# Prompt attention in another block order, and cached rope columns turned by VectorE instead of TensorE

## The chip, the cores and the metric

The kernel is one launch on one core of a Trainium2 chip, in 32-bit floating point. The metric is device time in microseconds (us), the median of three runs. Five engines work side by side and wait for each other through semaphores only: TensorE (PE in the profile; PEld are its weight loads), VectorE (DVE), ScalarE (ACT), GpSimd (POOL) and SyncE (SP), which issues most of the transfers.

## The reference, cut to what matters

One layer of a decoder: a prompt of 512 tokens and, beside it, 8 sequences with 4 new tokens each over 4096 cached ones. The change touches two parts of it.

```python
# prompt: causal attention, 8 heads, 128 queries at a time; 64 latent-derived + 32 rope dimensions
s = (einsum('bqhd,bkhd->bhqk', qn_b, k_nope) + einsum('bqhr,bkr->bhqk', qr_b, kr)) * MLA_SCALE
s = where(kpos <= qpos, s, -inf)
o = einsum('bhqk,bkhd->bqhd', softmax(s), v)
# new tokens: attention over the paged cache, rows of 256 latent + 32 rope numbers
past = cache_l[page_table].reshape(Bd, -1, 288)
s_past = einsum('bthc,bkc->bhtk', q_lat, past[..., :256]) + einsum('bthr,bkr->bhtk', q_rope, past[..., 256:])
p = softmax(concat([s_past, s_new]) * MLA_SCALE)
ctx = einsum('bhtk,bkc->bthc', p[..., :n_past], past[..., :256]) + (the new rows' part)
```

## The kernel before

Every engine runs one written-out program in order. After the input projection, the recurrent branch and the memory's keys and values, the program comes to the two stages of this change; behind them follow the output projection, the memory attention and the MLP. All weight products go through one helper (line 544), which splits each 32-bit operand in two parts and makes three products.

**Prompt attention.** The 8 heads are taken in four pairs, and each pair has 8 steps: for block i = 0, 1, 2, 3 of 128 queries first the even, then the odd head, so 32 steps n in all. Block i sees i + 1 key tiles of 128 keys, which sets the width of everything in its step (128 to 512 columns). TensorE's program for step n is: the scores of block n (line 816) into one of three PSUM banks, the transposes of the probabilities of block n-3 (line 824), into the banks `T_BANK` in turn, and, on every second step, the values of block n-5 for both heads (line 838, 64 columns for each head) into `O_BANK`. VectorE adds the causal mask on the diagonal tile (1827), takes the negated maximum (1828), and for the block before it the reciprocal of the sum (1833) and the scaling (1834). ScalarE makes the exponentials (1397) and copies the transposed probabilities of block n-3 to SBUF (1405). Three blocks of scores can be open at once, since the scores of n wait for the exponentials of n-3.

Between these lies other work, tied to the step number. `k_pair(j)` on TensorE makes the keys of the next pair of heads and `k_copy(j)` on ScalarE takes them to SBUF, both at the first step of a pair. At the end of a pair ScalarE casts the output (`act_hi`, line 1412) and VectorE makes the remainder (`act_lo`, line 1842), both in their step n = m + 6 for the pair's last block m. From step 18 on the work for the new tokens is mixed in: `absorb_turn` (TensorE, line 770, steps 18 to 24) turns the weights w_uk through one bank, which ScalarE empties into `wukT` (1416) before the next of four goes in; `absorb` (line 778, step 27) makes the latent queries; `new_rows` (lines 789 to 794, step 30) scores the new rows. VectorE clears `qropez` (line 1799) and fills it with the rope queries: 128 rows, 8 sequences x 128 columns, where rows 32j to 32j+31 hold a sequence's queries in columns 32j to 32j+31 and zeros elsewhere.

**The page loop.** The cache is gathered in 16 halves of a sequence (n = 0 to 15): an indirect transfer from GpSimd (line 479) brings 2048 rows of 288 numbers into one of four buffers `pg`, 16 rows to a partition. For each, TensorE runs `turn(n+1)`, `turn_p(n)`, `score(n+1)`, `values(n)`:

- `turn` transposes the page (line 865), nine tiles of four 128x128 transposes each, into the four banks of `gps` in turn; ScalarE (1430) copies the even tiles to SBUF and VectorE (1851) the odd ones. The first tile holds the rope columns, which GpSimd has packed into `ropc` (line 489) so that four groups of 32 numbers fill 128 rows; the other eight are the latent columns, for `cT`.
- `turn_p` transposes the probabilities (line 891), VectorE copies them (1868).
- `score` makes one product of `ropT` with the zero-padded `qropez` over 512 columns (line 876), which writes all 128 output rows, and adds eight products with 32 weight columns each (line 881), in four column tiles of the array, for the latent part.
- `values` makes 16 products of 256 columns in the same four tiles (line 901).

VectorE takes the maximum of the scores (1860, 1861), then copies its tiles of the next page. ScalarE makes the exponentials (1443). Each 32-bit product stands in the trace as two records (passes), each with its own weight load; a transpose stands as one.

The first page's tiles follow straight on the prompt attention; four of the banks come free from it one by one, each with a wait of its own:

```python
                    if k >= 4:
                        pe.wait_ge((g_ta, g_td)[k % 2], (k - 2) // 2 if k % 2 == 0 else (k - 3) // 2)
                    elif k != 2:
                        pe.wait_ge((at_pT, new_act, None, at_lo)[k], (4 * H, 2, None, 4)[k])
```

Of the kernel before, what the change touches and what calls it, by code (L numbers as in the profile page):

```python
# [14 lines left out]
F32 = mybir.dt.float32  # L15
# [53 lines left out]
MLP_AT = {m: i for i, m in enumerate(MLP)}  # L69

# [15 lines left out]
def build(nc, x_prompt, x_sample, cache_mla, cache_mem_k, cache_mem_v, state_lru_h, state_conv, page_table,  # L86
# [7 lines left out]
    with ctx:  # L94
# [103 lines left out]
        ropT = at("ropT", [128, 512], F32, M0 + 34816)  # L198
# [7 lines left out]
        ropc = at("ropc", [128, 4, 128], F32, M0 + 39488)  # L206
# [75 lines left out]
        ropc_ok = sem("ropc_ok")  # L282
# [168 lines left out]
        def _(pool):  # L451
# [31 lines left out]
            def rope_part(n):  # L483
                pool.wait_ge(page_in[n % 4], 16 * (n // 4) + 16)
                if n == 0:
                    pool.wait_ge(new_pe, 1)
                else:
                    pool.wait_ge(g_T, 9 * n - 8)
                nc.gpsimd.tensor_scalar(ropc[:, :, :].rearrange("p i (j r) -> p j i r", j=4),
                                        pg[n % 4][:, :, CR:ROW].rearrange("p (j i) r -> p j i r", j=4), 1.0, 1.0,  # L490
                                        ALU.mult, ALU.mult).then_inc(ropc_ok, 1)
            for u in range(U_MLP + len(MLP)):
                n = 384 if U_QU <= u < U_UV else 1024
                if u == U_OUT:
# [6 lines left out]
                    pool.wait_ge(tile_done, T_OUT)  # L501
                    pool.wait_ge(wk_T, 4)
# [28 lines left out]
        def _(pe):  # L531
# [275 lines left out]
            for n in range(4 * H + 5):  # L807
                if n < 4 * H:
                    h, i = 2 * (n // 8) + n % 2, n % 8 // 2
                    if n % 8 == 0 and n // 8 + 1 < 4:  # L810
                        k_pair(n // 8 + 1)
# [7 lines left out]
                if 0 <= m < 4 * H:  # L819
# [3 lines left out]
                    for kt in range(m % 8 // 2 + 1):  # L823
                        mm = nc.tensor.transpose(T_BANK[m % 2][:, 128 * kt:128 * kt + 128],
                                                 pb[m % 4][:, 128 * kt:128 * kt + 128], ident[:, :])
                    mm.then_inc(at_T, 1)
                m = n - 5
                if m >= 0 and m % 2:
                    j, i = m // 8, m % 8 // 2
# [19 lines left out]
            def turn(n):  # L849

                pe.wait_ge(page_in[n % 4], 16 * (n // 4) + 16)
                pe.wait_ge(ropc_ok, n + 1)
                for i in range(9):
                    k = 9 * n + i
                    if k >= 4:
                        pe.wait_ge((g_ta, g_td)[k % 2], (k - 2) // 2 if k % 2 == 0 else (k - 3) // 2)
                    elif k != 2:
                        pe.wait_ge((at_pT, new_act, None, at_lo)[k], (4 * H, 2, None, 4)[k])
                    for z in range(4):
                        if i == 0:  # L860
                            src = ropc[:, z, :]
                        else:
                            c, j = divmod(i - 1, 4)
                            src = pg[n % 4][:, 4 * j + z, 128 * c:128 * c + 128]
                        mm = nc.tensor.transpose(gps[:, (k + 1) % 4, 128 * z:128 * z + 128], src, ident[:, :])  # L865
                    mm.then_inc(g_T, 1)

            def score(n):
# [5 lines left out]
                k = 9 * n  # L874
                pe.wait_ge((g_ta, g_td)[k % 2], k // 2 + 1)
                nc.tensor.matmul(out, qropez[:, b, :], ropT[:, :], start=True, stop=False, skip_group_check=True)  # L876
                for c in range(2):
                    for j in range(4):
                        k = 9 * n + 1 + 4 * c + j
                        pe.wait_ge((g_ta, g_td)[k % 2], k // 2 + 1)  # L880
                        mm = nc.tensor.matmul(out[32 * j:32 * j + 32, :], qlat[:, c, b, :],  # L881
                                              cT[:, c, 512 * j:512 * j + 512], start=False, stop=(c == 1),
# [1174 lines left out]
```

## Time and profile before

| what | value |
|---|---|
| median of 3 runs | 1060.57 us (1059.52 to 1063.98) |
| the profiled execution | 1060.25 us, span of its trace 1058.1 us |
| PE busy | 1003.6 us, 95% of the span |
| DVE, ACT, POOL busy | 515.5, 303.5, 453.7 us |
| prompt attention | 218.8 to 284.0 us of the trace |
| page loop | 284.0 to 431 us |

A matmul's duration in the trace holds its way through the array, so that records overlap: the time of a row of matmuls is read from start to start. Idle time of an engine is given with what ended it.

### The profile page before, as it was taken

Reading aid. Unit: us, or ns where it says so; the run is one execution under the profiler, and the core shown is the slowest. Engines: PE = TensorE matmul, PEld = TensorE weight load, DVE = VectorE, ACT = ScalarE, POOL = GpSimd, SP = SyncE. Lnnn points to the kernel's source line nnn. Section 1 sums busy time; section 2 is a strip of 40 time slices with the busy share of each in tenths; the row PEclk is TensorE's granted clock in tenths of the full one; section 3 lists DMA queues with packets and bytes.
Section 4 is the critical chain, followed back from the end, with each engine's and each line's share of the span. In section 5 each row is a group of like instructions: output and inputs, shape, how many; then the busy total and the mean of one; then the engine's idle time right before and its main releaser. Section 6 shows DMA issues by size and latency. Waiting matters only on the chain.

```text
span 1058.1 us, 19047 instructions
## 1 busy us (share of the span) xinstructions
PE 1003.6 (95%) x8116; PEld 897.0 (85%) x8116; DVE 515.5 (49%) x723; ACT 303.5 (29%) x619; POOL 453.7 (43%) x297
## 2 busy tenths in 40 slices
PE   4999989888999999899999899999999999999997
PEld 4989888755666666699985599999999999999996
DVE  3889887567455555366135346441243134214413
ACT  5333256366334444112025312210020011001212
POOL 3545567600111111365510045565565565555651
PEclk9999999999899999999999999999999999999999
DMA  6423344520556664542267022332322323323222
GB/s 177 129 60 81 99 137 133 144 90 31 213 199 265 258 266 172 203 140 80 61 251 267 2 60 81 88 92 81 97 84 84 97 80 90 91 80 97 84 80 85
DMA packets 144009, 129.78 MB, mean 123 GB/s; under 512 B 13093, under 2 KB 136882, under 8 KB 140086
## 3 DMA queue, kind: packets, MB, share of 16 engines
q1 hardware_dynamic: 138344, 87.99, 27.8%
q0 software_dynamic: 2304, 37.75, 9.2%
q10 hardware_dynamic: 3278, 2.83, 0.8%
q8 instruction: 64, 1.05, 0.4%
q14 instruction: 19, 0.16, 0.0%
HBM read 123.53 MB, written 5.03 MB: 122 GB/s over the span
## 4 chain that ended last, share of the span: by engine, by line
PE 80%; DVE 11%; ACT 3%; issue 2%; DMA 1%; POOL 1%; ACTq 1%; DVEq 0%; POOLq 0%
PE gps L544 55%; PE gps L865 6%; PE aux L881 3%; PE aux L901 2%; PE gps L992 1%; PE gps L1067 1%; PE aux L876 1%; POOL wlo L474 1%; PE aux L816 1%; DVE q L1788 1%; PE aux L1005 1%; PE gps L668 1%; PE gps L838 1%; DMA wraw<-in_w_mem_v_dram 1%; PE aux L1026 1%
## 5 line engine op out<-in xcount | busy, mean ns | idle before, releaser
L544 PE MATMUL gps<-act_hi,whi 128*128 128x272 f32 x944 | 274.6, 291 | 6.4 <-DVE act_lo L1564 4.1
L544 PE MATMUL gps<-act_lo,whi 128*128 128x272 f32 x944 | 273.8, 290 | 0.0
L544 PE MATMUL gps<-act_hi,wlo 128*128 128x272 f32 x944 | 273.2, 289 | 0.0
L461 POOL TENSOR_SCALAR whi<-wraw 128x1024 fp32r<-128x1024 f32 (+1 forms) x110 | 114.7, 1043 | 368.8 <-PE gps L544 316.0
L464 POOL TENSOR_TENSOR wlo<-wraw,whi 128x1024 fp32r<-128x1024 f32 (+1 forms) x110 | 260.6, 2369 | 9.2
L544 PE MATMUL gps<-h_hi,whi 128*128 128x272 f32 x640 | 185.8, 290 | 0.0
L544 PE MATMUL gps<-h_lo,whi 128*128 128x272 f32 x640 | 185.2, 289 | 0.0
L544 PE MATMUL gps<-h_hi,wlo 128*128 128x272 f32 x640 | 184.7, 289 | 0.0
L544 PEld LDWEIGHTS gps<-act_hi,whi 128*128 128x128 f32 x944 | 178.7, 189 | 6.9 <-issue 5.1
L544 PEld LDWEIGHTS gps<-act_hi,wlo 128*128 128x128 f32 x944 | 178.7, 189 | 0.0
L544 PEld LDWEIGHTS gps<-act_lo,whi 128*128 128x128 f32 x944 | 178.5, 189 | 0.0
L1902 DVE TENSOR_TENSOR XT<-gps,XT 128x544 f32<-128x544 f32 x48 | 34.8, 725 | 181.5 <-PE gps L544 181.5
L544 PEld LDWEIGHTS gps<-h_hi,whi 128*128 128x128 f32 x640 | 120.7, 189 | 0.4
L544 PEld LDWEIGHTS gps<-h_hi,wlo 128*128 128x128 f32 x640 | 120.7, 189 | 0.1
L544 PEld LDWEIGHTS gps<-h_lo,whi 128*128 128x128 f32 x640 | 120.6, 188 | 0.0
L1510 ACT ACTIVATE ms<-mr 128x544 f32<-128x544 f32 x32 | 21.1, 660 | 287.2 <-DVE mr L1982 287.2
L479 POOL DMA_INDIRECT pg<-in_cache_mla_dram,idx x16 | 16.5, 1031 | 149.4 <-PE aux L901 88.0
L1988 DVE TENSOR_TENSOR act_lo<-ms,act_hi 128x544 fp32r<-128x544 f32 x29 | 58.7, 2024 | 40.8 <-ACT act_hi L1514 40.8
L865 PE MATMUL gps<-ident,pg 128*128 128x128 f32 x512 | 58.7, 273 | 0.0
L474 POOL TENSOR_TENSOR wlo<-wraw,whi 128x512 fp32r<-128x512 f32 x32 | 46.9, 1490 | 23.0 <-ACT whi L1220 23.0
L865 PEld LDWEIGHTS gps<-ident,pg 128*128 128x128 f32 x512 | 56.4, 142 | 0.2 <-DVE act_lo L1842 0.2
L1851 DVE COPY cT<-gps 128x512 f32<-128x512 f32 x64 | 44.2, 691 | 23.0 <-PE gps L865 23.0
(356 smaller groups left out, 1479.2 us busy)
## 6 DMA issues: line engine op xcount, KB each, us to landing
wraw<-in_w_up_dram SPq DMA_DIRECT2D x32, 512.0 KB, 4.1
wraw<-in_w_down_dram SPq DMA_DIRECT2D x32, 512.0 KB, 3.9
wraw<-in_w_in_dram SPq DMA_DIRECT2D x14, 512.0 KB, 3.9
kv<-in_cache_mem_k_dram SPq DMA_DIRECT2D x7, 1024.0 KB, 7.0
kv<-in_cache_mem_v_dram SPq DMA_DIRECT2D x7, 1024.0 KB, 12.6
wraw<-in_w_mem_k_dram SPq DMA_DIRECT2D x8, 512.0 KB, 4.0
wraw<-in_w_mem_v_dram SPq DMA_DIRECT2D x8, 512.0 KB, 3.8
wraw<-in_w_out_dram SPq DMA_DIRECT2D x8, 512.0 KB, 4.8
```

The lines of the kernel that those rows point to most:

```text
L461: nc.gpsimd.tensor_scalar(whi[:, slot, 0:n], wraw[:, slot, 0:n], 1.0, 1.0, ALU.mult, ALU.mult).then_inc(pool_step, 1)
L464: nc.gpsimd.tensor_tensor(wlo[:, slot, 0:n], wraw[:, slot, 0:n], whi[:, slot, 0:n].bitcast(F32), ALU.subtract).then_inc(w_ready, 1)
L474: ins = nc.gpsimd.tensor_tensor(wlo[:, slot, part], wraw[:, slot, part], whi[:, slot, part].bitcast(F32), ALU.subtract)
L479: nc.gpsimd.indirect_dma_start(pg[n % 4][:, :, :].rearrange("p k d -> p (k d)"), None, rows_of_pages, bass.IndirectOffsetOnAxis(ap=idx[:, ...
L544: mm = nc.tensor.matmul(out_of(a), w_of(w, k), x_of(x, k, part), start=(k == 0 and s == 0), stop=(k == k_tiles - 1 and s == 2))
L865: mm = nc.tensor.transpose(gps[:, (k + 1) % 4, 128 * z:128 * z + 128], src, ident[:, :])
L881: mm = nc.tensor.matmul(out[32 * j:32 * j + 32, :], qlat[:, c, b, :], cT[:, c, 512 * j:512 * j + 512], start=False, stop=(c == 1), skip_gr ...
L901: mm = nc.tensor.matmul(aux[32 * j:32 * j + 32, 3, 0:256], pTs[:, 128 * i + 32 * j:128 * i + 32 * j + 32], pg[n % 4][:, 4 * j + i, 0:CR], ...
L1510: nc.scalar.activation(ms[:, n % 2, :], mr[:, n % 2, :], ACT.Square).then_inc(mlp_sq, 1)
L1851: V.tensor_copy(dst, gps[:, (k + 1) % 4, :]).then_inc(g_td, 1)
L1902: step(V.tensor_tensor(x, gps[:, 2 * (t % 2):2 * (t % 2) + 2, 0:HALF], x, ALU.add))
L1988: V.tensor_tensor(hidden(n)[1], ms[:, n % 2, :], hidden(n)[0].bitcast(F32), ALU.subtract).then_inc(mlp_lo, 1)
```

## The change

The order of the query blocks in a pair of heads becomes 2, 3, 1, 0. The keys of the next pair are made at steps 3, 11 and 17 instead of 0, 8 and 16. ScalarE's cast of a pair's output comes one step later, VectorE's remainder two. The clearing of `qropez` goes from VectorE to GpSimd.

The rope columns no longer pass through TensorE: VectorE transposes them in 32x32 blocks from the page buffer to `ropT` (`rope_turned`), and GpSimd's packing falls away. A page has eight tiles left to turn. The rope score becomes 16 products of 128 columns with 32 weight columns, behind the latent ones, with an output pattern in four pieces of 32. The first page's tiles wait accordingly.

```diff
+ORDER = (2, 3, 1, 0)
-        ropT = at("ropT", [128, 512], F32, M0 + 34816)
+        ropT = at("ropT", [128, 16, 32], F32, M0 + 34816)
-        ropc = at("ropc", [128, 4, 128], F32, M0 + 39488)
@@ GpSimd
-            def rope_part(n):
-                pool.wait_ge(page_in[n % 4], 16 * (n // 4) + 16)
-                if n == 0:
-                    pool.wait_ge(new_pe, 1)
-                else:
-                    pool.wait_ge(g_T, 9 * n - 8)
-                nc.gpsimd.tensor_scalar(ropc[:, :, :].rearrange("p i (j r) -> p j i r", j=4),
-                                        pg[n % 4][:, :, CR:ROW].rearrange("p (j i) r -> p j i r", j=4), 1.0, 1.0,
-                                        ALU.mult, ALU.mult).then_inc(ropc_ok, 1)
                     pool.wait_ge(tile_done, T_OUT)
+                    nc.gpsimd.memset(qropez[:, :, :], 0.0).then_inc(pool_set, 1)
                     pool.wait_ge(wk_T, 4)
                     gather(1)
                     pool.wait_ge(ql_ps, 1)
                     gather(2)
-                    rope_part(0)
                     pool.wait_ge(at_lo, 4)
                     gather(3)
-                    for i in range(NH):
-                        if i + 1 < NH:
-                            rope_part(i + 1)
-                        if i >= 1 and i + 3 < NH:
-                            pool.wait_ge(g_V, i)
-                            gather(i + 3)
+                    for i in range(NH - 4):
+                        pool.wait_ge(g_V, i + 1)
+                        gather(i + 4)
@@ TensorE, prompt attention
-                    h, i = 2 * (n // 8) + n % 2, n % 8 // 2
-                    if n % 8 == 0 and n // 8 + 1 < 4:
+                    h, i = 2 * (n // 8) + n % 2, ORDER[n % 8 // 2]
+                    if n in (3, 11, 17):
                         k_pair(n // 8 + 1)
@@ TensorE, turn(n)
-                pe.wait_ge(ropc_ok, n + 1)
-                for i in range(9):
-                    k = 9 * n + i
+                for i in range(8):
+                    k = 8 * n + i
                     if k >= 4:
-                        pe.wait_ge((g_ta, g_td)[k % 2], (k - 2) // 2 if k % 2 == 0 else (k - 3) // 2)
-                    elif k != 2:
-                        pe.wait_ge((at_pT, new_act, None, at_lo)[k], (4 * H, 2, None, 4)[k])
+                        pe.wait_ge((g_ta, g_td)[k % 2], (k - 4) // 2 + 1)
+                    else:
+                        pe.wait_ge((at_pT, new_act, at_lo, at_lo)[k], (4 * H, 2, 3, 4)[k])
@@ TensorE, score(n)
-                nc.tensor.matmul(out, qropez[:, b, :], ropT[:, :], start=True, stop=False, skip_group_check=True)
                 for c in range(2):
                     for j in range(4):
-                        k = 9 * n + 1 + 4 * c + j
+                        k = 8 * n + 4 * c + j
                         pe.wait_ge((g_ta, g_td)[k % 2], k // 2 + 1)
...
+                pe.wait_ge(g_rope, n + 1)
+                for g in range(4):
+                    for j in range(4):
+                        mm = nc.tensor.matmul(
+                            out[32 * j:32 * j + 32, :].rearrange("p (i g k) -> p g i k", i=4, g=4)[:, g, :, :],
+                            qropez[:, b, 32 * g:32 * g + 32], ropT[:, 4 * j:4 * j + 4, :], start=False, stop=(g == 3),
+                            skip_group_check=True)
                 mm.then_inc(g_S, 1)
@@ ScalarE, prompt attention
-                    if n % 8 == 0 and n // 8 + 1 < 4:
+                    if n in (3, 11, 17):
                         k_copy(n // 8 + 1)
-                m = n - 6
+                m = n - 7
                 if m >= 0 and m % 8 == 7:
@@ VectorE, prompt attention
                 if n == 18:
                     dve.wait_ge(tile_done, T_UK + 4)
-                    step(V.memset(qropez[:, :, :], 0.0))
+                    dve.wait_ge(pool_set, 9)
-                m = n - 6
+                m = n - 8
                 if m >= 0 and m % 8 == 7:
@@ VectorE, page loop
+            def rope_turned(n):
+
+                dve.wait_ge(page_in[n % 4], 16 * (n // 4) + 16)
+                V.transpose(ropT[:, :, :], pg[n % 4][:, :, CR:ROW]).then_inc(g_rope, 1)
+
+            dve.wait_ge(at_pv, 2 * H)
+            rope_turned(0)
             turned(0)
...
                 if n < NH - 1:
+                    rope_turned(n + 1)
                     turned(n + 1)
```

## Rows read from the trace of the kernel before

**Rows 1.** The page: busy time of PE, and the chain that ended last.

```profile
PE 1003.6 (95%) x8116; PEld 897.0 (85%) x8116; DVE 515.5 (49%) x723; ACT 303.5 (29%) x619; POOL 453.7 (43%) x297
...
PE 80%; DVE 11%; ACT 3%; issue 2%; DMA 1%; POOL 1%; ACTq 1%; DVEq 0%; POOLq 0%
PE gps L544 55%; PE gps L865 6%; PE aux L881 3%; PE aux L901 2%; PE gps L992 1%; PE gps L1067 1%; PE aux L876 1%; POOL wlo L474 1%; PE aux L816 1%; DVE q L1788 1%; PE aux L1005 1%; PE gps L668 1%; PE gps L838 1%; DMA wraw<-in_w_mem_v_dram 1
```

**Rows 2.** Windows: stretch, length, busy PE, PEld, DVE, ACT, POOL, granted clock, DMA.

```profile
218.80:284.00 65.20, 56.46 (x381) 38.55 (x381) 44.46 (x142) 36.66 (x113) 2.49 (x3) 0.95 0.21 79
...
263.00:274.00 11.00, 11.00 (x61) 8.14 (x63) 4.38 (x14) 2.20 (x8) 0.94 (x1) 0.69 0.90 354
302.00:428.00 126.00, 125.91 (x1268) 85.53 (x1264) 64.42 (x105) 53.48 (x108) 25.44 (x29) 1.00 0.62 234
```

**Rows 3.** Timeline of one page in the loop: start us, duration us, instruction.

```profile
319.93 0.66 PE L865 MATMUL gps<-ident,ropc 128*128 128x128 f32 x4
...
321.06 0.69 DVE L1851 COPY cT<-gps 128x512 f32<-128x512 f32 x1 [1.84 <-PE gps L865]
...
323.68 0.69 DVE L1851 COPY cT<-gps 128x512 f32<-128x512 f32 x1 [0.18 <-PE gps L865]
...
323.92 0.60 PE L891 MATMUL aux<-ident,ps 128*128 128x128 f32 x4
...
324.36 1.02 PE L876 MATMUL aux<-ropT,qropez 128*128 128x512 f32 x2
...
325.31 1.93 PE L881 MATMUL aux<-cT,qlat 128*32 128x512 f32 x16
...
327.05 1.91 PE L901 MATMUL aux<-pg,pTs 128*32 128x256 f32 x32
...
328.03 0.15 DVE L1861 TENSOR_SCALAR nm<-sl 128x1 f32<-128x1 f32 x1
...
328.89 0.66 PE L865 MATMUL gps<-ident,ropc 128*128 128x128 f32 x4
```

**Rows 4.** Timeline: runs of short passes elsewhere, with few weight columns.

```profile
234.70 1.09 PE L838 MATMUL gps<-pT,vn 128*64 128x128 f32 x16
...
237.87 0.44 PE L838 MATMUL gps<-pT,vn 128*64 128x128 f32 x4
...
428.17 0.33 PEld L925 LDWEIGHTS aux<-sl,ident 128*32 128x32 f32 x8 [0.17 <-issue]
...
431.63 0.21 PE L938 MATMUL aux<-wt,ident 32*32 32x2 f32 x7
...
436.78 1.13 PE L962 MATMUL aux<-ctxa,wuv 128*64 128x32 f32 x32 [0.88 <-DVE ctxa L1893]
```

**Rows 5.** Line 1922: durations in ns (min, median, max) and form.

```profile
L1922 DVE RECIPROCAL rsn<-rsn x2: 3553/3553/3553, 495.2 to 664.1; 128x544 f32<-128x544 f32 x2
```

**Rows 6.** Timeline of the attention stage and the first page.

```profile
246.84 0.91 DVE L1799 MEMSET qropez<- 128x1024 f32 x1 [0.16 <-issue]
...
277.10 1.13 PE L816 MATMUL aux<-Kb,q 96*128 96x512 f32 x2
...
282.94 1.09 PE L838 MATMUL gps<-pT,vn 128*64 128x128 f32 x16 [0.46 <-ACT pT L1405]
...
284.70 0.69 DVE L1842 TENSOR_TENSOR act_lo<-gps,act_hi 128x512 fp32r<-128x512 f32 x1 [3.54 <-ACT act_hi L1412]
285.31 0.68 DVE L1851 COPY cT<-gps 128x512 f32<-128x512 f32 x1
```

**Rows 7.** Waits in the attention stage: total us, times, longest.

```profile
PEld gps L770 <- ACT wukT L1416: 3.6, 3, 1.5
...
DVE act_lo L1842 <- ACT act_hi L1412: 2.6, 3, 1.0
```

More of the change, by code:

```diff
@@ L822, in _ @@
                         pe.wait_ge(at_pT, m - 1)
-                    for kt in range(m % 8 // 2 + 1):
+                    for kt in range(ORDER[m % 8 // 2] + 1):
                         mm = nc.tensor.transpose(T_BANK[m % 2][:, 128 * kt:128 * kt + 128],
@@ L873, in score @@
                     pe.wait_ge(g_exp, n - 1)
-                k = 9 * n
-                pe.wait_ge((g_ta, g_td)[k % 2], k // 2 + 1)
-                nc.tensor.matmul(out, qropez[:, b, :], ropT[:, :], start=True, stop=False, skip_group_check=True)
                 for c in range(2):
                     for j in range(4):
-                        k = 9 * n + 1 + 4 * c + j
+                        k = 8 * n + 4 * c + j
                         pe.wait_ge((g_ta, g_td)[k % 2], k // 2 + 1)
-                        mm = nc.tensor.matmul(out[32 * j:32 * j + 32, :], qlat[:, c, b, :],
-                                              cT[:, c, 512 * j:512 * j + 512], start=False, stop=(c == 1),
-                                              skip_group_check=True)
+                        nc.tensor.matmul(out[32 * j:32 * j + 32, :], qlat[:, c, b, :],
+                                         cT[:, c, 512 * j:512 * j + 512], start=(c == 0), stop=False,
+                                         skip_group_check=True)
[5 more added lines that the diff above has]
+                            qropez[:, b, 32 * g:32 * g + 32], ropT[:, 4 * j:4 * j + 4, :], start=False, stop=(g == 3),
+                            skip_group_check=True)
                 mm.then_inc(g_S, 1)
@@ L1388, in _ @@
             k_copy(0)
-            for n in range(4 * H + 6):
+            for n in range(4 * H + 7):
                 if n < 4 * H:
-                    if n % 8 == 0 and n // 8 + 1 < 4:
+                    if n in (3, 11, 17):
                         k_copy(n // 8 + 1)
-                    w = 128 * (n % 8 // 2 + 1)
+                    w = 128 * (ORDER[n % 8 // 2] + 1)
                     act.wait_ge(at_nm, n + 1)
@@ L1424, in turned @@
             def turned(n):
-                for i in range(9):
-                    k = 9 * n + i
-                    if k % 2 == 0:
-                        act.wait_ge(g_T, k + 1)
-                        dst = ropT[:, :] if i == 0 else cT[:, (i - 1) // 4, 512 * ((i - 1) % 4):512 * ((i - 1) % 4) + 512]
-                        nc.scalar.copy(dst, gps[:, (k + 1) % 4, :]).then_inc(g_ta, 1)
+                for k in range(8 * n, 8 * n + 8, 2):
+                    act.wait_ge(g_T, k + 1)
+                    i = k % 8
+                    nc.scalar.copy(cT[:, i // 4, 512 * (i % 4):512 * (i % 4) + 512], gps[:, (k + 1) % 4, :]).then_inc(g_ta, 1)
             def keep_ctx(n):
@@ L1820, in absorbed @@
                     V.tensor_scalar(nmn[:, :], sn[:, 0, :], -1.0, None, ALU.mult).then_inc(new_dve, 1)
-            for n in range(4 * H + 6):
+            for n in range(4 * H + 8):
                 if n < 4 * H:
-                    w = 128 * (n % 8 // 2 + 1)
+                    w = 128 * (ORDER[n % 8 // 2] + 1)
                     dve.wait_ge(at_s, n + 1)
@@ L1845, in turned @@
             def turned(n):
-                for i in range(9):
-                    k = 9 * n + i
-                    if k % 2:
-                        dve.wait_ge(g_T, k + 1)
-                        dst = ropT[:, :] if i == 0 else cT[:, (i - 1) // 4, 512 * ((i - 1) % 4):512 * ((i - 1) % 4) + 512]
-                        V.tensor_copy(dst, gps[:, (k + 1) % 4, :]).then_inc(g_td, 1)
+                for k in range(8 * n + 1, 8 * n + 8, 2):
+                    dve.wait_ge(g_T, k + 1)
+                    i = k % 8
+                    V.tensor_copy(cT[:, i // 4, 512 * (i % 4):512 * (i % 4) + 512], gps[:, (k + 1) % 4, :]).then_inc(g_td, 1)
+            def rope_turned(n):
[3 more added lines that the diff above has]
+            rope_turned(0)
             turned(0)
```

23 lines of the change are left out of this document (10 added, 13 removed).

## The prediction

> **What bounds the kernel now.** I read the page first [rows 1]: TensorE (PE) is busy 95% of the span and carries 80% of the chain that ended last. A shorter VectorE (DVE) or GpSimd (POOL) instruction is therefore worth nothing unless PE waits for it. Over half of the chain is line 544, the weight products, which the change leaves alone. It touches two stages: the prompt attention (218.8 to 284 us) and the loop over 16 half-sequences of cached pages (284 to 431 us).
>
> The table by windows [rows 2] tells them apart. In the page loop PE is busy 125.91 of 126 us and DVE 64.42: PE is the bound, at the full clock. In the attention stage PE is busy 56.46 of 65.2 us and DVE 44.46: neither is full, so waits matter. In the 11 us from 263 to 274 the granted clock averages 0.69, so part of that stretch runs at 1.2 instead of 2.4 GHz.
>
> The timeline of one page [rows 3] is the page loop's price list, read from start to start on PE: turning nine tiles 3.99 us (319.93 to 323.92, 0.44 a tile), turning the probabilities 0.44, the rope score 0.95, the latent scores 1.74, the values 1.84. That makes 8.96 us a page.
>
> **Change 1, the rope columns leave TensorE's turning.** Each page loses one of nine tiles: -0.44 us. The POOL instruction that packed the rope columns goes too; POOL was behind nobody's wait here, so that is worth nothing, and its gathers still wait for the same values. In return DVE gets one 128x512 transpose a page, and the rope score, which was two PE passes over 512 columns with 128 weight columns, becomes 16 matmuls of 128 columns with 32 weight columns, so 32 passes, in four 32-column tiles of the array.
>
> *What 32 short passes cost.* The latent scores have the same four tiles with 512 columns: four rounds of four side by side in 1.74 us, 0.435 a round [rows 3]. The values have 256 columns: eight rounds in 1.84 us, 0.230 a round, where half of 0.435 would be 0.218. So a change of weights adds 0.012 us a round. For 128 columns the nearest row is line 838, with two tiles of 64 weight columns: 16 passes take 1.09 us and 4 take 0.44, so six rounds cost 0.65, 0.108 a round [rows 4]. A round of 128 columns with four tiles is then 0.108 to 0.121 us, and eight rounds 0.87 to 0.97. The old score's two passes were two rounds of 512, 0.87. (The rest of its 0.95, about 0.08, is the step from the whole array to tiles; it moves to the border between the probabilities' turn and the latent scores.) I take 0.12 us more. Can PE start passes that fast? 32 of them in 0.97 us are 30 ns each. Line 962 runs 32 passes in 1.13 us, of which the last is about 0.22: 29 ns each, with 64 weight columns. Line 938 runs 7 passes in 0.21 us, of which the last is 0.17 [rows 4]. So issue is not the limit. What no row shows is four tiles of 128 rows of the array with loads only 128 columns apart. The least it can cost is 0 over the old score; the most I price in the rivals, from the loads of line 925.
>
> *Here a rule speaks against the change.* The Trainium skill, "TensorE: Matmul & The Clock Gate", section "Part 3: Packing small matmuls", says that a weight load overlaps matmuls in flight only when its group of rows differs; these tiles all use all rows. By that rule each round would first wait for four loads, and the sum would be that of rival A below; this case's values loop disagrees, at 0.230 us a round.
>
> *The DVE transpose.* No transpose stands in the trace. The nearest rows are DVE's copies of 128x512, 0.69 us [rows 3]; the dearest DVE instruction for that many elements is the reciprocal, 3.55 us for 544 [rows 5]. Below 0.69 there is nothing to win, because it lies beside PE. I take 0.7. Its place: DVE ends the maximum's last step at 328.18 us, 0.71 before the next turning starts, and DVE's first copy stood 1.13 us after a turning's start. So DVE is free for 1.84 us, and 0.7 fits. Beyond 1.84 there is a cushion of about 0.4 until PE misses the bank; at 3.3 us (the reciprocal scaled to 512) PE would wait some 1.1 us a page. The Trainium skill, "VectorE: DVE Perf Modes", section "The three transpose paths", gives 311 ns for a 128x128 bf16 transpose in 32x32 blocks; four times that, as an estimate, is 1.24 us and also fits, so the sum by it is the same. The last latent tile's copy (3.75 to 4.44 us after the turning's start) is needed now about a rope score earlier, at 4.9 and later: still hidden, with 0.5 us left.
>
> *Sum per page*: -0.44 + 0.12 = -0.32, for 15 pages -4.8 us. The first page differs [rows 6]: there DVE has the last act_lo (284.70 to 285.39) and only then the transpose, so its first copy comes about 0.7 later than 285.31. PE wants that bank at the sixth tile and stands about 0.6; with a tile less (-0.44) the page costs about +0.2. Page loop: -4.6 us. With free short passes it is -6.8.
>
> **Change 2, the order 2, 3, 1, 0.** The work stays the same; its place changes. In the terms below a transposed tile is 0.11 us on PE (a quarter of a 0.44 turning), a 128x128 value round for both heads 0.22.
>
> *Drain.* Now the last step is a block of four tiles: from its scores (277.10) to the end of its values (282.94 + 1.09 = 284.03) it takes 6.9 us [rows 6], DVE and ScalarE (ACT) steps one behind the other. With a block of one tile each step shrinks; I get 3.4 us (score 0.2, DVE 0.6, ACT 0.5, DVE 0.5, turn and copy 0.6, values 0.4, and 0.6 of ACT's work on the new rows between). But the three larger blocks before it now lie ahead of that point: three more tiles of scores (0.64), eight of transposes (0.87), two of values (0.44), 1.9 us on PE. Net -1.6.
>
> *Fill.* The first steps are now wide; PE does 1.2 us more while it waits for others anyway, but the keys of pair 1, formerly built while ACT copied those of pair 0, now cost 1.4 us within it. I take -0.5 (bounds -1.2 and +1.0).
>
> *act_lo two steps later.* Three times DVE stood for ACT's act_hi, 2.6 us together [rows 7], with the causal add and maximum of the next block queued behind. Now ACT goes one step later and DVE two, so the stall goes. PE is what waits next for half of that time at most: -1.0 (bounds 0 and -2.6).
>
> *Pair 2.* DVE's 0.91 us memset goes to POOL [rows 6], which is only waiting there; ACT's cast leaves the steps in which PE waits for wukT (3.6 us in three waits [rows 7]). -0.9 together. Against it the last key pair comes a step later, right before the first wukT turn, which needs its bank: PE can stand there 0 to 1.2 us, I take +0.6.
>
> Sum: -1.6 - 0.5 - 1.0 - 0.9 + 0.6 = -3.4 us, bounds -7 and +2. The clock is an unknown in both directions: 31% of 11 us, so up to 3.4 us, hangs on the low stretch around the many small matmuls of line 778, which both kernels have.
>
> **Rivals.** *A, the loads of the short passes do not hide (slower).* Line 925's eight loads of 32 weight columns take 0.33 us, the last 0.11: 0.031 each [rows 4]. Four ahead of each round are 0.125, eight rounds 1.0 us. Page: -0.44 + 1.0 = +0.56, over 16 pages +9.0; with the attention's -3.4 it is +5.6, so 1066 us. For it: nothing with 128 columns and four tiles is in the trace. Against it: the same mechanism would make the values 8 x (0.218 + 0.125) = 2.7 us, and they take 1.84. It cancels the whole gain from a rope score of 1.52 us on, and makes the kernel measurably slower from 1.85. *B, the order gives nothing or harms:* the steps around wukT and the key copies stay what sets the pace and only move. Page loop -4.6, attention +1: 1057 us. For it: PE, DVE and ACT each wait for each other in this stage, so a shorter step can simply turn into another's wait. *C, everything hides and the clock stays up:* -6.8 - 3.4 - 2 to 3: 1048 us. *D, the transpose is slow:* at 2.65 us over my price it makes the page -0.32 + 1.1 = +0.8, thus +12 - 3.4: 1069 us; only if it were as dear as a reciprocal.
>
> **How the numbers follow.** The profiled execution took 1060.25 us; -4.6 - 3.4 gives 1052.25. It stands 0.32 below the median of the runs (1060.57), so 1052.6. Chances: forecast 0.60, B 0.14, C 0.10, A 0.12, D 0.04. The likeliest case's own range is 1049 to 1056. For 8 in 10 I leave out A and D at the top (0.16) and a little of C: 1047 to 1061. A measurement of this kernel can tell from no change about 0.5%, 5.3 us. The forecast is faster in nearly all of its 0.60 and C in all; B lies within 0.5%, with a piece of the forecast and part of A; A's other part and D are slower: faster 0.69, same 0.20, slower 0.11.
>
> **What would show it.** Right: the page period falls from 8.96 to about 8.6, nine groups of four transposes become eight, the rope score's passes start 27 to 31 ns apart, DVE's transpose is near 0.7 us and its first copy still comes about 1.1 us after the turning's start; attention ends its last value matmul near 280.6 instead of 284.0, act_lo no longer waits for act_hi in the loop. Wrong: passes of the rope score 45 ns apart or more; a turning that stands at its sixth tile for DVE; wukT waits longer than 3.6 us; a low clock that lasts beyond 10 us.

## The result: 1052.7 us, and the profile after

The changed kernel takes 1052.7 us (median of 8 runs, 1047.78 to 1055.11); the kernel before took 1060.53 in the same session (8 runs, 1055.33 to 1063.98). The ratio is 0.9922, 95% interval 0.9899 to 0.9944: faster by 0.8%. I had forecast 1052.6. The profiled execution took 1052.64 us with a span of 1050.5, against 1060.25 and 1058.1.

The page of the kernel after, busy times and the chain that ended last (as [rows 1]):

```profile
PE 1001.0 (95%) x8532; PEld 903.9 (86%) x8532; DVE 515.1 (49%) x730; ACT 299.6 (29%) x611; POOL 442.7 (42%) x282
...
PE 81%; DVE 11%; ACT 3%; issue 2%; DMA 2%; POOL 1%; ACTq 1%; DVEq 0%; POOLq 0%
```

PE's busy time fell by only 2.6 us for a span 7.6 us shorter. So part of the gain is removed waiting, and busy time hides a clock effect. Windows of the kernel after, by stage: ahead of attention, attention up to the absorb products, from there to the first page, page loop, from the fold to the next stage (107.8 us), and the rest; then three stretches at the low clock:

```profile
0.00:218.60 218.60, 192.25 (x1387) 175.66 (x1387) 158.31 (x180) 96.02 (x184) 120.28 (x89) 0.99 0.45 125
...
218.60:262.10 43.50, 39.70 (x270) 26.73 (x270) 35.21 (x114) 29.72 (x88) 1.90 (x2) 1.00 0.07 24
262.10:280.79 18.69, 18.18 (x119) 14.60 (x118) 8.08 (x28) 7.18 (x26) 0.94 (x1) 0.73 0.57 224
280.79:422.50 141.71, 139.59 (x1882) 101.19 (x1880) 80.75 (x139) 56.56 (x114) 18.99 (x17) 1.00 0.60 229
...
422.50:530.30 107.80, 103.75 (x856) 101.82 (x857) 43.44 (x39) 12.60 (x19) 50.31 (x29) 0.98 0.38 118
530.30:1050.50 520.20, 507.50 (x4026) 483.87 (x4026) 189.32 (x231) 97.52 (x181) 250.34 (x144) 1.00 0.33 100
...
265.90:272.90 7.00, 7.00 (x35) 5.27 (x35) 4.20 (x14) 3.40 (x10) 0.94 (x1) 0.53 0.79 289
276.00:280.00 4.00, 4.00 (x31) 2.92 (x30) 2.20 (x9) 1.60 (x8) 0.00 (x0) 0.59 0.01 2
429.00:433.00 4.00, 3.14 (x14) 3.17 (x15) 0.29 (x1) 0.17 (x1) 0.00 (x0) 0.57 0.97 304
```

The same stages before, in windows with their borders at the same instructions:

```profile
218.80:262.90 44.10, 37.13 (x250) 24.19 (x250) 35.37 (x116) 29.22 (x90) 0.94 (x1) 1.00 0.05 16
262.90:284.00 21.10, 19.32 (x133) 14.35 (x132) 9.09 (x27) 7.44 (x24) 1.56 (x2) 0.84 0.54 212
284.00:431.50 147.50, 145.90 (x1464) 98.53 (x1462) 76.91 (x131) 61.18 (x122) 29.46 (x32) 1.00 0.57 220
...
431.50:537.90 106.40, 102.45 (x857) 100.59 (x858) 43.81 (x40) 12.60 (x19) 50.31 (x29) 1.00 0.37 119
```

The difference adds up: -0.2 ahead of attention, -3.0 in attention (-0.6 and -2.4), -5.8 in the page loop, +1.4 after the fold, 0.0 in the rest: -7.6 us. My terms were -4.6 and -3.4, and nothing after the fold. That the total lies within 0.1 us of the forecast is luck: a page loop better than forecast paid for something that I had not forecast, low clock at two new places (276 to 280 and 429 to 433 us). It is luck too that the stretch ahead of attention, which the change hardly touches, is as long in both profiles: over the thirteen profiles of this case it runs from 216.1 to 222.3 us (more on that in the last section).

**The page loop.** Timeline of one page after, as [rows 3]:

```profile
323.53 0.70 DVE L1842 STREAM_TRANSPOSE ropT<-pg 128x512 f32<-128x512 f32 x1
...
324.32 3.71 PE L850 MATMUL gps<-ident,pg 128*128 128x128 f32 x32
...
325.45 0.69 DVE L1837 COPY cT<-gps 128x512 f32<-128x512 f32 x1 [1.22 <-PE gps L850]
...
327.87 0.60 PE L881 MATMUL aux<-ident,ps 128*128 128x128 f32 x4
...
328.40 1.92 PE L864 MATMUL aux<-cT,qlat 128*32 128x512 f32 x16
...
330.14 1.06 PE L870 MATMUL aux<-ropT,qropez 128*32 128x128 f32 x32
330.14 0.79 PEld L870 LDWEIGHTS aux<-ropT,qropez 128*32 128x32 f32 x28 [0.30 <-issue]
...
331.01 1.91 PE L891 MATMUL aux<-pg,pTs 128*32 128x256 f32 x32
...
332.85 0.87 PE L850 MATMUL gps<-ident,pg 128*128 128x128 f32 x6
```

From start to start on PE: turning 3.55 (was 3.99), probabilities 0.53 with the step to tiles, latent scores 1.74, rope score 0.87, values 1.84: 8.53 us a page, was 8.96. The 32 short passes take 0.87 us, 27 ns each, which is what the two long passes streamed. DVE's transpose is 0.70 us, and the first DVE copy still comes 1.13 us after the turning's start.

**Attention's end.** Timeline of the kernel after, from the last score on, as [rows 6]:

```profile
275.61 0.58 PE L806 MATMUL aux<-Kb,q 96*128 96x128 f32 x2
...
277.77 0.15 DVE L1821 RECIPROCAL sm<-sm 128x1 f32<-128x1 f32 x1
...
280.42 0.44 PE L828 MATMUL gps<-pT,vn 128*64 128x128 f32 x4 [0.34 <-ACT pT L1395]
280.79 4.20 PE L850 MATMUL gps<-ident,pg 128*128 128x128 f32 x32
...
281.52 0.69 DVE L1830 TENSOR_TENSOR act_lo<-gps,act_hi 128x512 fp32r<-128x512 f32 x1 [2.95 <-ACT act_hi L1402]
282.13 0.70 DVE L1842 STREAM_TRANSPOSE ropT<-pg 128x512 f32<-128x512 f32 x1
```

From the last score to the first page's turning: 5.2 us, was 6.9, forecast 3.4 (at the full clock, in f3 below, it is 4.1). The only act_lo that waits for act_hi is the last one; the three waits inside the loop [rows 7] are gone.

### The profile page after: what moved, and what is told of

The parts are those of the page before. It is cut to its first block, busy times and chain, and to the rows that moved or that the text cites. A ratio compares the mean times of both kernels' runs of the same rounds, so it can differ in the third digit from the quotient of the medians.

```text
span 1050.5 us, 19847 instructions
## 1 busy us (share of the span) xinstructions
PE 1001.0 (95%) x8532; PEld 903.9 (86%) x8532; DVE 515.1 (49%) x730; ACT 299.6 (29%) x611; POOL 442.7 (42%) x282
## 4 chain that ended last, share of the span: by engine, by line
PE 81%; DVE 11%; ACT 3%; issue 2%; DMA 2%; POOL 1%; ACTq 1%; DVEq 0%; POOLq 0%
PE gps L534 56%; PE gps L850 5%; PE aux L864 3%; PE aux L891 2%; PE aux L806 1%; PE gps L982 1%; PE gps L1057 1%; PE aux L870 1%; DMA wraw<-in_w_mem_v_dram 1%; DVE q L1776 1%; PE gps L828 1%; POOL wlo L476 1%; PE aux L995 1%; PE aux L1016 1%; PE aux L881 1%
## 5 line engine op out<-in xcount | busy, mean ns | idle before, releaser
L1498 ACT ACTIVATE ms<-mr 128x544 f32<-128x544 f32 x32 | 21.1, 660 | 287.2 <-DVE mr L1976 287.2
L1837 DVE COPY cT<-gps 128x512 f32<-128x512 f32 x64 | 44.1, 690 | 25.9 <-PE gps L850 25.7
```

The source lines that it names most:

```text
L1498: nc.scalar.activation(ms[:, n % 2, :], mr[:, n % 2, :], ACT.Square).then_inc(mlp_sq, 1)
L1837: V.tensor_copy(cT[:, i // 4, 512 * (i % 4):512 * (i % 4) + 512], gps[:, (k + 1) % 4, :]).then_inc(g_td, 1)
```

## Experiments

Below, "first" is attention from its first score to the absorb products, "second" from there to the first page, with the granted clock behind it. Both are read from windows of each profile.

**e1, attention alone.** The kernel before with the order 2, 3, 1, 0, the later key pairs, the later act_lo and the memset on POOL, and the old page loop:

```diff
-                    h, i = 2 * (n // 8) + n % 2, n % 8 // 2
-                    if n % 8 == 0 and n // 8 + 1 < 4:
+                    h, i = 2 * (n // 8) + n % 2, ORDER[n % 8 // 2]
+                    if n in (3, 11, 17):
```

> The kernel before with the attention part of the change alone (order 2, 3, 1, 0, keys at steps 3, 11, 17, cast and remainder later, clearing on GpSimd); the page loop is the old one. My theory, two gains that add: the page period stays 8.96 us, the attention stage (first score to first page tile) is about 62 us instead of 65.2, and the kernel is 2 to 3.5 us faster than before. Rival, the page part carries all and the attention part only shifted waits: within 1 us of before. Rival, the two parts need each other (VectorE's later remainder delays the first page): slower than before.

1057.82 us (12 runs, 1055.4 to 1060.93), ratio 0.9974 [0.9958, 0.9990]: -2.7 us. First 43.5, second 17.9 (clock 0.73), page loop 147.7, fold to the next stage 109.0. That is within my 2 to 3.5 us. Its profile, of one of its slowest runs (1060.87 us), has low clock at four places from 214 us on, so it can't price the attention part.

**e2, page loop alone.** The changed kernel with all of attention as before:

```diff
-ORDER = (2, 3, 1, 0)
+ORDER = (0, 1, 2, 3)
-                m = n - 8
+                m = n - 6
-                    dve.wait_ge(pool_set, 9)
+                    step(V.memset(qropez[:, :, :], 0.0))
```

> The changed kernel with the old attention (order 0, 1, 2, 3, keys at steps 0, 8, 16, cast and remainder at their old steps, clearing on VectorE) and the new page loop. My theory: the page period is 8.53 us as in the changed kernel, the attention stage 65.2 us as before, and the kernel 5.5 to 6.5 us faster than before. Rival, the period depends on how the stage before ends: another period than 8.53. Rival, the fold stage behind the loop falls to the low clock because the page loop has changed: 4.5 to 5 us faster only, with a granted clock under 1 at the start of the output projection.

1052.87 us (6 runs, 1051.24 to 1054.58), ratio 0.9931 [0.9907, 0.9956]: -7.3 us. Its page loop is 141.6. That is more than the 5.5 to 6.5 that I expected. The two parts alone add to -10.1 and together give -8.2, which the intervals allow; but at the medians the attention part on top of the new page loop shows nothing (1052.87 and 1052.7). Its profile says where to look: first 44.1, as before, second 19.4 at a clock of 0.91 (before: 21.1 at 0.84), and 107.8 from the fold to the next stage, the rival's low clock.

**e3 and e4, the attention part in halves.** e3 is the changed kernel with `ORDER = (0, 1, 2, 3)` and all other places new; e4 has the new order, and the key pairs, act_lo, act_hi and memset at their old places.

> The changed kernel with ORDER = (0, 1, 2, 3) and nothing else undone. If the order of the blocks is the cause of the attention's gain, the stage goes back to about 65 us and the kernel is 2.5 to 3 us slower than the changed one. If the places of the keys, of the cast and remainder and of the clearing are the cause (rival), it stays within 1 us of the changed one. My sum gave the order 2.1 of 3.4 us, so I expect about 64 us for the stage, 1.5 to 2 us slower.

> The changed kernel in the order 2, 3, 1, 0, but with keys at steps 0, 8, 16, cast and remainder at step m + 6, clearing on VectorE. If the order alone is the cause, the attention stage stays at about 62.3 us and the time within 0.5 us of the changed kernel. My sum gave these places 1.3 of 3.4 us: about 63.5 us for the stage and 1 to 1.5 us slower than the changed kernel, with VectorE waiting about 1 us for act_hi three times again.

e3: 1052.73 us (8 runs), ratio 0.9929 [0.9905, 0.9953]. e4: 1052.71 us (8 runs), ratio 0.9926 [0.9894, 0.9957]. I had expected e3 1.5 to 2 us and e4 1 to 1.5 us slower than the changed kernel; in the run times neither half can be seen. In the profiles both can. Windows, first and second, of e3, then of e2:

```profile
216.70:258.20 41.50, 37.28 (x256) 25.70 (x256) 34.28 (x115) 28.96 (x88) 1.92 (x2) 1.00 0.12 46
258.20:277.60 19.40, 17.73 (x132) 13.17 (x131) 8.88 (x27) 7.85 (x26) 0.94 (x1) 0.91 0.57 228
...
216.10:260.20 44.10, 37.13 (x250) 24.18 (x250) 35.38 (x116) 29.24 (x90) 0.94 (x1) 1.00 0.11 40
260.20:279.60 19.40, 17.63 (x132) 13.24 (x131) 9.07 (x27) 7.43 (x24) 0.94 (x1) 0.91 0.58 231
```

Against e2, at the same clocks, the new places take 2.6 us out of the first part. There PE's waits for DVE's scaled probabilities fall from 1.8 us to next to nothing and those for ScalarE's exponentials from 0.8 as well, while the wait for wukT, which the memset and the cast were to shorten, falls only from 2.8 to 2.5. Which of the moved places did it was not taken apart. Against e3, the changed kernel's first part is 2.0 longer, because the new order puts more of PE's work ahead of the absorb products (39.70 us busy against 37.28), and its second part gets that back, if the clock lets it. e4's first part is 46.1 us at a clock of 0.96, its second 17.9 at 0.72: it has low stretches in three places from 253 to 284 us, and DVE waits for act_hi three times again, 3.2 us together.

**e6, passes of 64 columns.** The rope score in 64 passes instead of 32, the same columns in all:

```diff
-                        mm = nc.tensor.matmul(
-                            ..., ropT[:, 4 * j:4 * j + 4, :], start=False, stop=(g == 3),
+                    for half in range(2):
+                        for j in range(4):
+                            mm = nc.tensor.matmul(
+                                ..., ropT[:, 4 * j + 2 * half:4 * j + 2 * half + 2, :],
```

> The changed kernel with the rope score cut once more: 32 products of 64 columns (64 passes) instead of 16 of 128 (32 passes); the same columns stream. It measures where a pass is too short for its weight load, rival A of the prediction. If loads of 32 columns hide fully, the rope score stays 0.87 us (13.6 ns a pass) and the page period 8.53 us. If a load of 32 weight columns costs the 31 ns apart that line 925 of the kernel before showed, 64 of them take 2.0 us and the period becomes about 9.65 us. If the floor is 15 ns a pass (half of line 962's 29 ns for 64 weight columns), it is 0.96 us and the period 8.6 us; this is what I expect.

One run, 1050.52 us. Timeline of PE in e6:

```profile
319.47 1.92 PE L864 MATMUL aux<-cT,qlat 128*32 128x512 f32 x16
321.21 1.08 PE L871 MATMUL aux<-ropT,qropez 128*32 128x64 f32 x64
322.11 1.91 PE L892 MATMUL aux<-pg,pTs 128*32 128x256 f32 x32
```

64 passes with 64 weight loads take 0.90 us: 14 ns each. Twice the loads cost 0.03 us a page, where 64 loads at rival A's price of 0.031 would take 2 us.

**e7, a transpose four times as long.** It measures how much DVE time fits ahead of the turning. The repeats write the same values:

```diff
-                V.transpose(ropT[:, :, :], pg[n % 4][:, :, CR:ROW]).then_inc(g_rope, 1)
+                for z in range(4):
+                    ins = V.transpose(ropT[:, :, :], pg[n % 4][:, :, CR:ROW])
+                    ...
```

> The changed kernel with VectorE's transpose of the rope columns written four times over for each page (the first three are repeats whose result is overwritten by the same values): 2.8 us instead of 0.7 ahead of VectorE's first copy of a page. My theory of the slack: VectorE is free for 1.84 us before its first copy and TensorE has a cushion of about 0.4 us more, so of the 2.8 us about 0.5 to 0.6 us stand open on TensorE, once a page, at the second or third tile of the turning that needs VectorE's bank: period 8.53 -> 9.0 to 9.1 us, page loop 141.7 -> about 150, time about 1061. Rival: the slack is larger, because VectorE only has to follow ScalarE's alternate banks: then the period stays below 8.7 and the time below 1055.

One run, 1062.74 us. Timeline of a page in e7:

```profile
319.06 2.40 PE L850 MATMUL gps<-ident,pg 128*128 128x128 f32 x20
...
321.13 1.25 DVE L1837 COPY cT<-gps 128x512 f32<-128x512 f32 x2
...
321.83 1.53 PE L850 MATMUL gps<-ident,pg 128*128 128x128 f32 x12 [0.38 <-DVE cT L1837]
...
327.39 2.94 DVE L1843 STREAM_TRANSPOSE ropT<-pg 128x512 f32<-128x512 f32 x4
...
328.19 2.08 PE L850 MATMUL gps<-ident,pg 128*128 128x128 f32 x17
```

The period is 9.13 us, 0.60 more, the upper end of what my slack theory gave (0.5 to 0.6). DVE's first copy comes 2.07 us after the turning's start, 0.94 late, of which PE's bank buffers took 0.34 (I had 0.4). PE stops at the sixth tile, as I had said for a slow transpose, not at the second or third, as this expectation had it. The page loop took 155.3 us, not 150: the first two turnings, up to the first turn of probabilities, took 18.4 us instead of 13.0, since there four transposes lie open behind the last act_lo and behind other DVE work, and the clock was at half from 282 to 286 us.

**s1 and s3, thinning out the narrow products.** If the low clock comes of the many small absorb products in one block, spreading them over four steps (s1), and the new rows' scores over two (s3 in addition), should keep it up.

```diff
-                if n == 27:
-                    absorb()
+                if 26 <= n <= 29:
+                    absorb(n - 26)
```

> The changed kernel with the 32 passes of line 768 (latent queries), which stand as one block of 3.8 us in step 27, spread over steps 26 to 29, 8 in each, and VectorE's copy of them moved from step 28 to 29. Theory: in that block VectorE and ScalarE starve (VectorE waits over 3 us) and the few columns let the clock fall right after. Spread, the attention stage should take 58 to 60 us instead of 62.2, with a shorter low stretch. Rival, the attention stage at this point is bound by TensorE alone: the same 62 us, since the work is the same.

> The kernel above, and the new rows' scores (2.9 us in step 30) also split, one half in step 30, the other in 31. Theory: another 0.5 to 1 us less in the stage than the kernel above, 57.5 to 59 us. Rival, the second half now delays the last blocks' transposes, and the drain is longer: no gain over the kernel above.

s1: 1055.54 us (9 runs, 1049.85 to 1061.37), ratio 0.9977 [0.9950, 1.0004]. s3: 1058.87 (10 runs), ratio 0.9995 [0.9967, 1.0024]. Both are worse than the changed kernel. The profiled execution of s1 was its best: attention 59.6 us, inside my 58 to 60, but at a clock of 1.00 throughout, and f3 below takes the same 59.6 at 0.97. Over its nine runs the mean clock went from 0.994 (1049.85 us) to 0.981 (1061.37 us). The profile of s3, whose attention took 69.0 us where I had 57.5 to 59, shows the other end, window and clock:

```profile
262.50:286.00 23.50, 23.39 (x113) 18.83 (x111) 8.04 (x27) 6.60 (x23) 0.94 (x1) 0.50 0.37 146
```

PE stays at 1.2 GHz for 23.5 us. The theory fell: spreading the narrow work does not keep the clock up, and in this one profile of s3 it stays down longer than in any other.

**f1, f2, f3, filler products.** They go the other way: dead 128x128 products of ones, written to an unused bank, in the places where PE is narrow or waits: 7 at the new rows' scores and 14 in the waits of the fold. So that the bank is free, PE also waits for an exponential ahead of the new rows' scores, and for the last page's copies in the fold.

```diff
+            def hold(count, out):
+                for _ in range(count):
+                    nc.tensor.matmul(out, ident[:, :], ones[:, :], start=True, stop=True)
...
+            hold(4, gps[:, 3, 0:128])
             pe.wait_ge(fold_dve, 3)
```

f1 has both groups, f2 is f1 with the old order of the blocks, f3 has only the fold's 14.

> The changed kernel with idle work on TensorE that changes no result: 7 products of 128 columns into a free bank beside the new rows' scores (0.21 us each at the full clock, mostly in waits of 0.3 to 0.5 us), and 14 in the waits of the fold stage behind the page loop. Theory: all three kernels with the order 2, 3, 1, 0 show a second low-clock stretch near 276 to 283 us of the trace and the kernels with the order 0, 1, 2, 3 do not, and most show one at the start of the output projection; it is the light work there that lets the clock fall, and each us at 1.2 GHz costs half a us. If so, the granted clock stays 1.00 in 273 to 285 us and in the 14 us after the fold starts, the mean clock of the run rises from 0.989 to about 0.993, and the kernel is 2 to 3 us faster than the changed one, near 1049.5 us. Rival, the clock falls whatever stands there: the clock is unchanged and the kernel 0.5 to 1.5 us slower by the added work.

> The changed kernel with the old order of the query blocks (0, 1, 2, 3) and with the 21 filler products of the version before (7 at the new rows' scores, 14 in the waits of the fold). Theory that the order gives nothing that outlasts the clock: the same time as with the new order and the fillers, 1050 us within 1.5 us either way. Rival, that the order is worth its 1.9 us at full clock once the fillers hold the clock: 1052 us or more, and a mean clock no lower than with the new order.

> The changed kernel with the 14 filler products in the fold's waits alone, none in the drain of attention. If the gain of 2.6 us comes from the low stretch at 429 to 433 us, that at the start of the output projection, this keeps about 1.5 us of it: 1051.2 us, and the profile shows the fold at the full clock and the second low stretch of the drain (276 to 280 us) back. If all of it comes from the drain, it is 1052.7 us, as without fillers; if the drain's fillers cost as much as they give back, 1050 us.

| kernel | median us (6 runs) | range | ratio to before |
|---|---|---|---|
| f1 | 1050.05 | 1048.18 to 1052.94 | 0.9916 [0.9890, 0.9943] |
| f2 | 1050.98 | 1049.07 to 1054.75 | 0.9913 [0.9884, 0.9942] |
| f3 | 1049.42 | 1048.16 to 1052.21 | 0.9901 [0.9872, 0.9930] |

Windows of f3, fold to the next stage, and from the last score to the first page:

```profile
420.90:527.30 106.40, 105.21 (x881) 103.35 (x882) 43.52 (x40) 12.60 (x19) 50.35 (x29) 1.00 0.38 120
...
275.18:279.31 4.13, 3.54 (x37) 2.44 (x36) 2.21 (x9) 2.07 (x10) 0.00 (x0) 1.00 0.03 11
```

The fold's fillers cost nothing (they stand in waits for DVE) and the 1.4 us are back in all three. That the fillers did it is not shown: without any, the same stretch took 106.3 to 106.4 us at a clock of 1.00 in before, e6, s1 and s3, and 107.7 to 109.1 at 0.97 to 0.98 in the changed kernel, e1, e2, e3, e4 and e7. The drain's fillers, with their wait, cost time: at a clock of 0.97 attention takes 61.3 us in f1 and 59.6 in f3, and 62.5 in f2 and 60.9 in e3. The second low stretch of the drain did not show in f3, against my expectation, though its attention is the changed kernel's to the instruction: whether the clock falls there differs from one execution to the next. f2 came out within my 1.5 us of f1: the order is not seen to be worth anything in run times. f3 is the best version found, about 3 us under the changed kernel; the intervals of the two ratios overlap, so that lead is likely, not certain.

## Why the prediction was right, point by point

**Turned tile, -0.44 a page: right.** 3.99 to 3.55.

**Short passes, +0.12 a page: the term that was mis-sized.** They measured 0.87 us, the lower end of my bounds. My lower row, 0.108 a round from two tiles of 64 weight columns, was the nearer one. The 0.012 a round that I took from the values loop isn't a cost of changing weights for shorter rounds: with sixteen rounds of 64 columns (e6) the whole excess is 0.03. That makes the period -0.43 instead of -0.32 us, over thirteen full periods and the last page's own -0.4 together -5.9. (My -6.8 for free short passes was a slip: -4.6 less 16 times 0.12 is -6.5.) Rival A needed a rope score of 1.52 us even to cancel the gain; the 0.87 and e6's 0.90 refute it. The Trainium skill, "TensorE: Matmul & The Clock Gate", section "Part 3: Packing small matmuls", says that a weight load overlaps matmuls in flight only when its group of rows differs. Here the trace disagrees: 28 loads on all rows lie within the 0.87 us of their 32 matmuls.

**Transpose 0.7, hidden: right,** and so was the slack behind it (e7). The Trainium skill's figure in "VectorE: DVE Perf Modes", section "The three transpose paths", would have made it 1.24 us as an estimate; this fp32 one took 0.70, a copy's time. Rival D is out.

**First page, +0.2: wrong sign, -0.1.** From the first turning to the second it took 8.99 us after and 9.10 before. The mechanism is there (PE 0.34 short of DVE's bank, behind act_lo and the transpose), only cheaper, as the short passes also save there. What I left out is the loop's other ends. The second page saved nothing (8.94 us against 8.96): its turning took 3.96 us against 3.98, since PE stood 0.19 for an ACT copy in it. And the last page up to the fold took 0.2 more, where one DVE instruction needed 0.65 us instead of 0.22 (below). So the loop gave -5.9 - 0.1 + 0.2, the -5.8 of the windows, against -4.6.

**Attention, -3.4: the sum holds, the split doesn't.** At like clocks, e2 63.5, e3 60.9 and f3 59.6 us (all 0.97): the places are worth -2.6, where I had -1.0 - 0.9 + 0.6 = -1.3; the order -1.3, where I had -1.6 - 0.5 = -2.1. So -3.9, of which the changed kernel's own profile shows -3.0, because the second low stretch takes its part. f1 against f2 gives the order a second time, 61.3 and 62.5 us: -1.2.

Windows from the last score to the first page, of e3 and then of f3, and f3's timeline in its window:

```profile
270.75:277.62 6.87, 5.37 (x53) 3.76 (x52) 3.00 (x9) 3.14 (x10) 0.00 (x0) 1.00 0.01 4
...
275.18:279.31 4.13, 3.54 (x37) 2.44 (x36) 2.21 (x9) 2.07 (x10) 0.00 (x0) 1.00 0.03 11
...
275.71 0.30 DVE L1826 TENSOR_TENSOR aux<-aux,causal 128x128 f32<-128x128 f32 x1 [3.42 <-PE aux L811]
...
276.63 0.19 ACT L1398 ACTIVATION_READ_ACCUMULATOR pb<-aux,sm 128x1 f32 x1
276.64 0.68 DVE L1841 TENSOR_TENSOR act_lo<-gps,act_hi 128x512 fp32r<-128x512 f32 x1
...
277.24 0.15 DVE L1832 RECIPROCAL sm<-sm 128x1 f32<-128x1 f32 x1
```

In the order, the term that was mis-sized is the drain: it shrinks by 2.7 us, from 6.87 to 4.13, where I had 3.5, down to 3.4. The work that moves ahead of it, 5.37 - 3.54 = 1.8 us on PE, is what I had (1.9), and all that lies ahead of the last score grows by only 1.4, so 0.4 of it fell into waits, near my 0.5 for the fill. Of the 0.7 that the drain takes more, 0.3 lies between the score's start and DVE's first step, 0.53 us where I had put 0.2. The other 0.4 is a step that I had missed: the act_lo of the pair before, put two steps later, now lies between the last block's maximum and its reciprocal, which starts at 277.24 where ScalarE was done at 276.82. In the changed kernel's own drain, with the low clock, this step is covered: DVE's scaling ends at 278.24, PE's slowed matmuls keep it busy until it comes to that block at 278.88, and the whole takes 5.2.

**What hangs on the clock.** I had called it an unknown of both signs around one block, up to 3.4 us. It is more places than one: the block at 266 to 273 us, the drain, and the fold. Runs of one kernel differ with it: e4 from 1048.87 us at a mean clock of 0.992 to 1058.17 at 0.984, about 1.2 us for 0.001; s1 from 0.994 to 0.981, 11.5 us. Half the clock for 2.1 us lowers the mean over 1050 us by 0.001 and loses 1.05 us of PE's work, so this is what a kernel bound by PE should show. It isn't all: of the changed kernel's eight runs, 1047.78 and 1052.64 us both have 0.990, and 1055.11 has 0.989. The 2.6 us wait ahead of attention (last section) comes and goes as well. My "wrong" sign, a low clock beyond 10 us, came true in part: 7 + 4 us in attention, 4 after the fold. Spreads of this size cover attention's halves in run times, and rival B (the order harms or gives nothing) is neither shown nor refuted there; profiles at like clocks, two pairs with one profile for each kernel, speak against it by 1.2 to 1.3 us. Rival C, everything hides and the clock stays up, 1048 us, is what f3 comes near to (1049.42), with the loads hidden and the fold at the full clock.

**What stays open.** Why the clock falls after the fold in six of the ten profiles without fillers (the changed kernel, e1 to e4, e7) and not in the other four (before, e6, s1, s3). It isn't the page loop: e1 has the old one and falls, e6, s1 and s3 have the new one and don't. Whether the fold's fillers prevent it, or their three profiles were three good ones, would take more profiles of the changed kernel and of f3. So the +1.4 us is what this profile shows and not a cost proven of the change. And how often the 2.6 us wait comes in each kernel's runs isn't known, so how much of e2's -7.3 us is that, against the -5.9 of its page loop, is not settled.

## What to carry to other kernels

Price a stage's work from start to start on the bounding engine and keep the granted clock beside it; compare two kernels at like clocks only. Before a cause is given for something that one profile shows, look whether the other profiles of the same stretch show it too. When an instruction is moved out of a wait, look where it lands: here act_lo left the loop's waits and came to lie in the chain of the last block. Splitting a streaming matmul into short tiled passes was free here down to 128 columns, and nearly so at 64, with the same columns streamed in all.

## What the runs showed of the hardware

**Short passes.** Four tiles of 32 columns in the array take a pass every 27 ns with 128 columns and every 14 ns with 64, loads included; nothing shorter was tried.

**VectorE waits for GpSimd.** Timeline of the kernel after, end of the page loop:

```profile
418.67 2.36 POOL L466 TENSOR_TENSOR wlo<-wraw,whi 128x1024 fp32r<-128x1024 f32 x1
...
420.46 0.65 DVE L1870 TENSOR_TENSOR wt<-ml,mx 32x72 f32<-32x72 f32 x1
```

The same DVE instruction takes 0.22 us in before, e1 and e7, where it starts at most 0.05 us ahead of the end of such a POOL instruction or after it, and 0.47 to 0.65 in e2, e3, f3 and here, where it ends 0.08 us after POOL's. The eight DVE adds of q just ahead of attention show it in large, in the group by line of the kernel after and of e2:

```profile
L1776 DVE TENSOR_TENSOR q<-qr,ntq 32x544 f32<-32x544 f32 x8 | 12.9, 1616 | 0.3
```

```profile
L1775 DVE TENSOR_TENSOR q<-qr,ntq 32x544 f32<-32x544 f32 x8 | 8.7, 1090 | 0.3
```

One add takes 0.72 us alone and up to 2.78 beside POOL's subtractions. In e2 the four copies of the keys behind the adds are the slower ones instead (4.4 us against 1.5), but nobody waits for those. For the adds somebody does, as the waits in the kernel after show, just ahead of attention:

```profile
ACT vn L1360 <- DVE q L1776: 4.3, 1, 4.3
...
PE gps L534 <- ACTq L1361: 2.6, 1, 2.6
```

ScalarE's copy of a tile waits for the last add, and PE for its bank. This 2.6 us wait of PE stands in seven profiles (before, after, e1, e4, f2, f3, s1), in which the adds take 12.2 to 12.9 us and attention starts at 218.6 to 222.3; it is missing in the six others (e2, e3, e6, e7, f1, s3), with 8.7 to 10.2 us and starts from 216.1 to 217.6. The Trainium skill, "SBUF — State Buffer", section "SBUF: two separate sides", says that a VectorE instruction with two SBUF inputs and a GpSimd instruction that reads SBUF lock each other out for the whole instruction; the first row and the adds agree.

**Clock and narrow work.** PE's record is busy for 4.00 of 4.00 us at 276 to 280 and the granted clock is still 0.59. Over one and the same stretch the clock falls in one execution and not in another: the drain's instructions are the same in f3 (1.00) and the changed kernel (0.67 from the last score to the first page). With fillers of 128 columns the fold's stretch stood at 1.00 in three profiles of three, without them in four of ten; in the one profile of s3, which spreads the narrow products, the clock was 0.50 for 23.5 us.
